# Other slots for the mixing stage's steps, and a half-chunk grid with narrow splits for the hybrid-head stage

## The reference

```
first block, per layer:
  h = h + 0.5 * rms_norm(swiglu(rms_norm(h)))            # width 2816
  u = rms_norm(h);  a_b, a_c, a_x, b_u, c_qkv, d_qkv, d_f, gates = split(u @ w_in)
  y_a = (a_b * conv3(a_c * a_x)) @ w_a                   # short convolution
  y_b = silu(layer_norm(conv31(glu(b_u)) + b)) @ w_b     # 31 taps, depthwise
  y_c = differential attention(c_qkv), 4 heads x 2 maps, rms_norm per head, @ w_c
  y_d = forgetting attention(d_qkv, cumsum(log_sigmoid(d_f))), 8 heads, @ w_d
  h = h + rms_norm((sum of sigmoid(gate_i) * y_i) @ w_o)
  h = h + 0.5 * rms_norm(swiglu(rms_norm(h)))
second block ("hybrid heads"), per layer:
  z = rms_norm(h) @ w_in                                 # 2656 columns
  a: 6 query, 2 key heads, rms_norm per head, axial rope, dense attention
  b: 6 query, 2 key heads, rope, window of 128 and a sink
  c: latents of 192 and 128, normed, times w_uq and w_ukv, 4 heads of 64 + 32 rope
  h = h + (concat(a, b, c) * silu(gates)) @ w_out
result: rms_norm(h)
```

## Time and profile before

| | |
|---|---|
| median of 3 runs | 1870.01 us (1867.84 to 1870.3) |
| profiled execution | 1870.01 us, its span 1868.2 us |
| PE busy | 1731.6 us, 93% of the span |
| DVE busy | 1125.2 us, 60% |
| ACT busy | 794.7 us, 43% |
| mean granted TensorE clock | 0.961 |

### The profile page before, as it was taken

How to read it: one execution, slowest core, us unless ns; L and a number is a source line. 1 busy time by engine, 2 the same in 40 slices (tenths; PEclk the granted TensorE clock), 3 DMA queues, 4 the chain that set the end, 5 groups by cost and what they waited for, 6 DMA issues and landing times.

```text
span 1868.2 us, 28467 instructions
## 1 busy us (share of the span) xinstructions
PE 1731.6 (93%) x12340; PEld 1614.7 (86%) x12340; DVE 1125.2 (60%) x1317; ACT 794.7 (43%) x1011; POOL 41.1 (2%) x64
## 2 busy tenths in 40 slices
PE   7999988888999999999998888899999998889886
PEld 6999888878999999899988778899999997669765
DVE  5444666766766544744466676676545476647663
ACT  5334544333444443543363443344534444434532
POOL 0000000000000000000000000000000010001000
PEclk9999999989999999999999998999999999889978
DMA  7555543433455555555454332354655452215310
GB/s 280 182 184 188 193 181 122 150 113 136 159 180 203 183 192 189 190 192 188 181 199 162 136 139 110 137 179 158 220 186 181 180 210 96 88 59 203 113 45 23
DMA packets 43357, 299.43 MB, mean 160 GB/s; under 512 B 4816, under 2 KB 5216, under 8 KB 8416
## 3 DMA queue, kind: packets, MB, share of 16 engines
q1 hardware_dynamic: 39744, 285.23, 42.2%
q10 hardware_dynamic: 3488, 12.38, 1.9%
HBM read 296.52 MB, written 1.06 MB: 159 GB/s over the span
## 4 chain that ended last, share of the span: by engine, by line
PE 74%; DVE 10%; ACT 8%; issue 5%; DVEq 3%; POOL 1%; DMA 1%; POOLq 0%; ACTq 0%; SPq 0%
PE ps L1373 21%; PE ps L1374 21%; PE ps L1375 21%; DVE wlo L838 3%; ACT whi L536 3%; PE ps L1744 2%; PE ps L1771 2%; DVEq L1119 1%; ACT prob L726 1%; ACT prob L808 1%; PE ps L1459 1%; PE ps L1755 1%; POOL rs L497 1%; PE ps L1460 1%; PE ps L1417 1%
## 5 line engine op out<-in xcount | busy, mean ns | idle before, releaser
L838 DVE TENSOR_TENSOR wlo<-raw,whi 128x2048 fp32r<-128x2048 f32 x270 | 616.8, 2291 | 474.8 <-ACT whi L536 468.2
L1373 PE MATMUL ps<-xhi,whi 128*128 128x256 f32 (+1 forms) x2512 | 724.6, 288 | 0.0
L1374 PE MATMUL ps<-xlo,whi 128*128 128x256 f32 (+1 forms) x2512 | 716.9, 285 | 0.0
L1375 PE MATMUL ps<-xhi,wlo 128*128 128x256 f32 (+1 forms) x2512 | 716.5, 285 | 0.0
L536 ACT ACTIVATE whi<-raw 128x2048 fp32r<-128x2048 f32 x270 | 508.2, 1905 | 17.5 <-DMA raw<-stream 17.0
L1373 PEld LDWEIGHTS ps<-xhi,whi 128*128 128x128 f32 (+1 forms) x2512 | 487.1, 194 | 6.2 <-issue 2.9
L1374 PEld LDWEIGHTS ps<-xlo,whi 128*128 128x128 f32 (+1 forms) x2512 | 486.7, 194 | 3.1 <-issue 0.6
L1375 PEld LDWEIGHTS ps<-xhi,wlo 128*128 128x128 f32 (+1 forms) x2512 | 486.0, 193 | 0.4
L1373 PE MATMUL ps<-whi,yar 128*128 128x512 f32 (+1 forms) x492 | 195.9, 398 | 0.7 <-DVE wlo L838 0.7
L1374 PE MATMUL ps<-wlo,yar 128*128 128x512 f32 (+1 forms) x492 | 192.1, 391 | 0.0
L1375 PE MATMUL ps<-whi,yar 128*128 128x512 f32 (+1 forms) x492 | 191.6, 389 | 0.0
(11 more groups left out here) (203 smaller groups left out, 1745.5 us busy)
## 6 DMA issues: line engine op xcount, KB each, us to landing
raw<-stream SPq DMA_DIRECT2D x270, 1024.0 KB, 4.8
gpre<-pre_gain ACTq DMA_DIRECT2D x9, 512.0 KB, 4.2
gpost<-post_gain ACTq DMA_DIRECT2D x6, 512.0 KB, 5.3
mix<-cum ACTq DMA_DIRECT2D x2, 1024.0 KB, 6.7
h<-x_in SPq DMA_DIRECT2D x2, 512.0 KB, 5.9
out<-mix SPq DMA_DIRECT2D x4, 256.0 KB, 2.1
cst<-cst_in ACTq DMA_DIRECT2D x1, 704.0 KB, 11.8
cst<-cst_in ACTq DMA_DIRECT2D x1, 576.0 KB, 5.7
```

What stands on the lines that cost most here:

```text
L838: TT(wlo[:, s, :], raw[:, s, :], whi[:, s, :].bitcast(F32), ALU.subtract).then_inc(lo_v, 1)
L1373: pe.matmul(dst, lh, rh, start=first, stop=False)
L1374: pe.matmul(dst, lh, rl, start=False, stop=False)
L1375: return pe.matmul(dst, ll, rh, start=False, stop=last)
```

## The change

It has two parts. **Mixing stage:** the load order `COLS` brings chunk 22 (the forget logits) to slot 6, and most steps get other slots: the 31 taps are spread over slots 6 to 33 instead of 6 to 36, so three slots hold two of them; the f_ steps come earlier, the attention groups and flips at other distances, the layer norm steps two slots earlier. Branch c's output moves out of `thb`. **Hybrid stage:** the table is now in half chunks (28 halves and four output steps), chunks 5, 6, 7 come before 3 and 4 (`HCOLS`), DVE's split is a step of its own (`split`, in the second half of each slot, two chunks ahead), all splits and loads take only the columns that a chunk uses (`chunk_width`: 1536, 1280, 768 or 512 of 2048), ACT takes over squares, the copies of chunks 2, 4, 7 and the value copies, the rotations take fewer instructions, group 9 has no buffers of its own, w_out's first token half is accumulated in banks 0 and 1 chunk by chunk, and the norms' scratch has columns of its own.

```diff
-COLS = (14, 15, 0, 1, 2, 3, 10, 11, 12, 13, 22, 4, 5, 6, 7, 8, 9, 16, 17, 18, 19, 20, 21)
+COLS = (14, 15, 0, 1, 2, 3, 22, 10, 11, 12, 13, 4, 5, 6, 7, 8, 9, 16, 17, 18, 19, 20, 21)
+HCOLS = (0, 1, 2, 5, 6, 7, 3, 4, 8, 9, 10, 11, 12, 13)
...
-        at(6 + tap, "conv", tap)
+        at(6 + tap * 28 // B_CONV, "conv", tap)
...
-    for g, s in enumerate((10, 12, 15, 17, 21, 24, 26, 29)):
+    for g, s in enumerate((12, 14, 16, 18, 22, 24, 27, 29)):
         at(s, "scores", g)
         at(s + 1, "weigh", g)
         at(s + 2, "turn", g)
         at(s + 3, "values", g)
...
-HYB_V = (2, 4, 7) + GATES
+HYB_V = GATES
...
+SLOTS2 = ((5.5, 6.5), (6.5, 7.5), (7.5, 8), (8, 9), (9, 10), (10, 10.5), (10.5, 11.5), (11.5, 13), (13, 14), (14, 15))
...
+    for g, (a, b) in enumerate(SLOTS2):
+        at(a, "scores", g)
+        at(a, "exp", g)
+        at(a, "weigh", g)
+        at(b, "turn", g)
+        at(b, "values", g)
...
+    for p in range(1, 15):
+        at(p + 0.5, "split", p + 2)
...
+        def acc_bank(X, t):
+            return 4 * t if X >= 3 * DEPTH else 4 + 2 * t
...
-                sp.dma_start(raw[:, c % SLOTS, :], stream[LOAD[c]]).then_inc(landed[c % SLOTS], 16)
+                w = chunk_width(c)
+                sp.dma_start(raw[:, c % SLOTS, 0:w], stream[LOAD[c]][:, 0:w]).then_inc(landed[c % SLOTS], 16)
...
-                A(whi[:, s, :], raw[:, s, :], ACT.Copy).then_inc(hi_ready, 1)
+                w = chunk_width(ch)
+                A(whi[:, s, 0:w], raw[:, s, 0:w], ACT.Copy).then_inc(hi_ready, 1)
...
+                    elif kind == "values":
+                        g = step[1]
+                        br, t, kv, ne = group(g)
+                        if br < 2:
+                            act.wait_ge(o_done, l * GROUPS2 + (8 * DEPTH + g + 1))
+                            rows_ = slice(64 * kv, 64 * kv + 64)
+                            A(oAB[rows_, 3 * br:3 * br + 3, t * P:(t + 1) * P],
+                              bank(3)[rows_, 0:3 * P].rearrange("p (m t) -> p m t", m=3), ACT.Copy).then_inc(o_read, 1)
...
-                            TT(prob[:, 0:ne, :], sc, win[:, t, :].unsqueeze(1).to_broadcast([P, ne, T]), ALU.add)
+                            far = slice((1 - t) * P, (2 - t) * P)
+                            TT(sc[:, :, far], sc[:, :, far], win[:, t, far].unsqueeze(1).to_broadcast([P, ne, P]), ALU.add)
...
-                        if turned:
+                        if turned and w == 1 and t == 1:
                             pe.wait_ge(y_ready, l * 4 + turned)
...
+                    if kind == "out":
+                        j = step[1]
+                        ready(wo[j])
+                        pe.wait_ge(y_ready, l * 3 + (4 * DEPTH + (1, 2, 2, 3)[j]))
...
+                        _, p, i, half = step
+                        c = ch + p
+                        if p < 2 or half and i in (AT_UQ, AT_UKV):
                             continue
-                        ready(c)
+                        if half == 0:
+                            ready(c)
+                            hyb_free(pe, l, p)
```

More of the change, by code:

```diff
@@ L180, in at @@
     def at(slot, *step):
[L181 to L191, removed]
+        before.setdefault(int(2 * slot), []).append(step)
+    at(3, "a_norm")
+    at(4.5, "flip", 0)
+    at(5, "flip", 1)
+    at(6, "b_rotate")
+    at(8.5, "flip", 2)
+    at(8.5, "flip", 3)
+    at(8, "l_norm")
+    at(9.5, "l_turn")
     at(11, "cq_rotate")
     at(12, "ck_rotate")
[L194 to L199, removed]
-    at(12, "o_gate", 0)
-    at(15, "o_gate", 1)
-    at(17, "o_gate", 2)
-    rank = {"flip": 0, "l_turn": 0, "turn": 1, "scores": 2, "exp": 2, "values": 3, "weigh": 4}
-    steps = []
[L205 to L208, removed]
+    at(12, "flip", 4)
+    at(12, "flip", 5)
+    at(12.5, "flip", 6)
+    at(12.5, "flip", 7)
+    for g, (a, b) in enumerate(SLOTS2):
[4 more added lines that the diff above has]
+        at(b, "values", g)
+    at(12, "o_gate", 0)
+    at(14, "o_gate", 1)
+    at(15.5, "o_gate", 2)
+    for p in range(1, 15):
+        at(p + 0.5, "split", p + 2)
+    rank = {"flip": 0, "l_turn": 0, "turn": 1, "scores": 2, "exp": 2, "values": 3, "split": 7, "weigh": 8}
+    steps = []
+    for half in range(2 * AT_WOUT + 4):
+        steps += sorted(before.pop(half, []), key=lambda x: rank.get(x[0], 6))
+        if half < 2 * AT_WOUT:
+            steps.append(("chunk", half // 2, HCOLS[half // 2], half % 2))
+        else:
+            steps.append(("out", half - 2 * AT_WOUT))
     assert not before, before
@@ L572, in boundary @@
                     squares_acc(X, ch, 1, 0)
+                else:
+                    split(ch + 1)
                 if not last:
@@ L862, in boundary @@
                 split(ch)
-                split(ch + 1)
-                per = 4 if share else 2
                 if share:
+                    split(ch + 1)
                     dve.wait_ge(gpost_in, X * 16 + 16)
@@ L875, in boundary @@
                                 dve.wait_ge(sq_done, q + (4 * t + 1))
-                            STT(out=thb[:, half], in0=bank(4 + 2 * t + n), scalar=share, in1=gpost[:, half], op0=ALU.mult,
+                            STT(out=thb[:, half], in0=bank(acc_bank(X, t) + n), scalar=share, in1=gpost[:, half], op0=ALU.mult,
                                 op1=ALU.mult)
@@ L1204, in _ @@
+                dve.drain()
                 for step in HYB:
                     kind = step[0]
-                    if kind == "chunk":
-                        i = step[1]
-                        c = ch + i
-                        if i in GATES:
+                    if kind == "split":
+                        split(ch + step[1])
+                    elif kind == "chunk":
+                        _, p, i, half = step
+                        c = ch + p
+                        if i in GATES and half:
@@ L1420, in turns, with rows_of, rows_tail @@
                         ins.then_inc(xt_done, 1)
-            def rows_tail(X, chs, lhs, lls, wait, last=False):
+            def rows_of(X, ch, lh, ll, t, final, first, last=False):
+                s = ch % SLOTS
+                wh, wl = wts(whi, s, 2), wts(wlo, s, 2)
+                for a in range(2):
+                    if final and t and a and not last:
+                        turns(X + 1, 0)
+                    for b in range(2):
+                        n, k = (a, b) if final else (b, a)
+                        ins = mm3(bank(acc_bank(X, t) + n), lh[:, k, t * P:(t + 1) * P], ll[:, k, t * P:(t + 1) * P],
+                                  wh[:, k, n * 512:(n + 1) * 512], wl[:, k, n * 512:(n + 1) * 512], first and k == 0,
+                                  final and b == 1)
+                    if final and not (t and a):
+                        ins.then_inc(acc_done, 1)
+                if t:
+                    ins.then_inc(used, 1)
+            def rows_tail(X, chs, lhs, lls, wait):
                 for t in range(NT):
@@ L1665, in _, with banks_free @@
                 token_pair(ch, X, Z_CHUNKS[0])
+                wo = [ch + AT_WOUT + i for i in range(4)]
+                def banks_free(step, wanted):
+                    at = HYB.index(step)
+                    for b in wanted:
+                        users = [x for x in HYB[:at] if x[0] == "l_turn" or x[0] == "flip" and 2 + x[1] % 2 == b
+                                 or x[0] == "values" and b == 3]
+                        if not users:
+                            continue
+                        if users[-1][0] == "l_turn":
+                            pe.wait_ge(lat_ready, l + 1)
+                        elif users[-1][0] == "flip":
+                            pe.wait_ge(qkt_a, l * 8 + (users[-1][1] + 1))
+                        else:
+                            pe.wait_ge(o_read, l * GROUPS2 + (8 * DEPTH + users[-1][1] + 1))
```

342 lines of the change are left out of this document (168 added, 174 removed).

## The result

The changed kernel takes 1796.66 us (median of 4, 1791.93 to 1797.79), the one before 1869.4 us (median of 4, 1867.84 to 1870.3). The ratio is 0.9607, with a 95% interval of 0.9588 to 0.9625: 73 us less, where 1800 us was forecast. The profiled execution took 1796.47 us, its span is 1794.7.

What follows compares the result with a forecast made beforehand. PE was taken as the bound: its matmuls, its waits and the time a lowered clock adds. Gains of 42 us in two mixing layers and 28 in two hybrid layers, 70 from 1870.0, gave 1800 us, range 1760 to 1832.

Steps and rivals of the forecast that it cites:

- the clock's share: Time PE loses to a lowered clock before the change: 11 us per mixing layer, 12 per hybrid layer.
- The mixing layer, 43 to 22: Mixing layer's idle time plus clock loss falls from 43 us to 22: 21 won, 42 in two layers.
- turn 2: Mixing stage, slot 17: PE waits 5.0 us because DVE is behind with `weigh` and the read of `values` 1.
- turn 3: Mixing stage, after slots 17 and 18: PE waits 5.8 us, from full DVE slots plus 3.7 waiting for ACT.
- gate: Mixing stage, slot 23: the first gate waits 4.4 us for ACT's copy of slot 22's chunk to free bank 0.
- The hybrid layer, 37 to 22: Hybrid layer's idle time plus clock loss falls from 37 us to 22: 14 to 15 won, 28 in two layers.
- ukv: Hybrid stage: this chunk waits 3.9 us for ACT's copy of uq, which stands behind exp 6.
- turns 3 and 5: Hybrid stage: new PE waits of 1.0 us each at these two turns.
- The waits dissolve: Rival, both stages: a quarter of the new waits remains, with most low clock gone; 1762 us, chance 0.25.
- Only the mixing stage pays: Rival, hybrid stage: uq, ukv and the end eat the hybrid gain; 1828 us, chance 0.13.
- ScalarE becomes the bound: Rival, hybrid layers: ACT's added work makes later chunks wait for their banks; 1879 us, slower, chance 0.03.
- The hybrid clock stays low: Rival, hybrid stage: small transposes and score products keep the clock low, 12 us stay; 1810 us, chance 0.08.

Runs made afterwards that it cites:

- e7: Changed kernel with ACT's exps of groups 2 to 4 and o_norm behind their slot's copy and split, and no taps in slots 15 to 19: 1758.21 us.
- e6: Changed kernel with the convolution taps moved out of slots 15 to 19, more of them in slots 6 to 11: 1787.53 us.
- e2: Changed kernel with the mixing stage's edits taken back, so only the hybrid part is changed: 1837.08 us.
- e8: Changed kernel with the edits of e7 and e4, and w_out's last split on DVE moved to slot 14.5: 1746.58 us.
- e4: Changed kernel with ACT's copies of the uq and ukv chunks, and the split behind, moved to their slot's first half: 1790.66 us.

## Why the prediction was right

**What can be won.** I had put the clock's share of a mixing layer at 11 us and its idle time at 32, so 43 to win. e7 shows the floor: at a clock of 1.00 the layer's matmuls take PE 318.3 us, and before it was busy 329.5, so the clock cost 11.3; idle was 362.2 - 329.5 = 32.7. Both terms stand.

**The mixing layer, 43 to 22.** Idle after is 339.7 - 322.8 = 16.9 in layer 0 and 15.5 in layer 1 (15.5 forecast); the clock costs 322.8 - 318.3 = 4.5 and 7.5 (6.5 forecast). Wait by wait in layer 0: turn 0 1.22 (1.1), turn 1 0.92 (0.7), turn 2 4.80 (5.0), turn 3 4.87 (5.8), gate 4.58 (4.4). The one that missed is turn 3's, by 0.9. The five add up to 16.4, between the 17.0 of the plain sum and the 15.5 that I took. My sum for turn 3 counted DVE's load beside ACT's order; e6 shows that without the load 4.7 of the 4.9 us stay.

**The hybrid layer, 37 to 22.** Idle fell from 24.6 to 164.6 - 147.6 = 17.0, where I took 15; PE's busy time fell by 6.9, where I took 5 for the clock. The two errors cancel, which is luck. The idle time came out low because I subtracted 0.3 for each of 14 waits from a list of 19 (it has 13 waits and adds up to 18.6), and because a wait of 0.86 for the norm at the layer's start, there before and after, was not on it. Of that list, ukv 3.79 (3.9), `flip` 5 2.75 (2.7), chunk 5 1.73 (1.8), out 3 1.83 (2.0) and out 1 1.26 (1.1) stand. **A step that was wrong:** turns 3 and 5 (1.0 each) do not wait at all and turn 2 only 0.48 instead of 0.9, perhaps because I counted DVE's half slots as serial where the half slot between has room, which no run tests; values 7 and 8 are 0.2 longer each. That is 2.4 us less and 0.4 more. There is luck in the total too: each part alone won more than I had for it (44.5 for 42, 32.7 for 28), while both together gave 4 us less than the two alone, of which 2.3 lie in hybrid layer 0 and its clock.

**The rivals.** *The waits dissolve* fell: every large one is there, within a us. That they could be dissolved, by another order, e7 shows: a mixing layer of 323.4 us, 38.8 less than before, with order changed, a buffer moved and some semaphore waits moved or weakened. *Only the mixing stage pays* fell by e2, 32.7 us. *ScalarE becomes the bound* fell: ACT is busy 80.9 of 164.6 us, and in that stage only uq's and ukv's copies hold up a chunk (3.79 and 0.46). *The hybrid clock stays low* fell: the layer's clock rose from 0.90 to 0.95, and to 0.97 in e8, while it has the same 937 PE instructions, its transposes among them. Of the 12 us that I had for the clock, PE's busy time lost 6.9 with the change and 10.6 in e8 (154.5, 147.6, 143.9). From the full change to e8 even the order of PE's instructions is the same, and only its waits differ. So most of the low clock before was due to the waits. The Trainium skill ("TensorE: Matmul & The Clock Gate", Part 4: PE-mode transpose) says that transposes do not count as work for the clock gate like other matmuls; by that rule the 12 us of the rival would have stayed, and the trace does not agree. What no run separates is whether transposes make the stage more sensitive to a short wait.

## What to carry over

When engines run in order, ask of each instruction that waits (an exp for a maximum) what is queued behind it that doesn't need it: here the copy that frees a PSUM bank and the split of the next chunk. In the mixing layers putting these ahead was worth 25 us, spreading DVE's load 6, both together 34, and in the hybrid stage narrower splits were worth nothing. Compare kernels stage by stage: the totals held another 4 to 5 us from stages whose code was the same. The account of idle time plus low clock, each read off whole stages, gave the total within 4 us, and a slot-by-slot sum gave every wait of a strict bank to 0.3 us; sums over waits that slack may absorb mostly came out too long.

## What the hardware showed that I had not expected

**Equal waits leave unequal stretches of low clock.** `turn` 2 waits 4.80 us in both mixing layers of the changed kernel. Eleven us around it in layer 0 and in layer 1, the same code:

```profile
321.00:332.00 11.00, 8.47 (x56) 7.34 (x57) 10.44 (x19) 1.08 (x2) 0.00 (x0) 0.84 0.18 73
1042.00:1053.00 11.00, 8.12 (x44) 6.99 (x45) 10.46 (x18) 1.43 (x2) 0.00 (x0) 0.69 0.19 81
```

A mean of 0.84 over 11 us, with levels of 1 and 1/2, is 3.5 us at 1.2 GHz; 0.69 is 6.8. PE then comes 1.1 us later to `turn` 3 in layer 1 and waits 1.1 us less there (3.79 for 4.87). Around that turn the means are 0.84 and 0.69 again, so the shorter wait has the longer stretch. Two times 3.3 us more at 1.2 GHz, half of it lost, are about what layer 1 lost more to the clock than layer 0 (7.5 us for 4.5).

**The same short wait was followed by low clock in one kernel and not in another.** Two stretches of 8 us of the changed kernel: `values` 4 waited 1.04 us in the hybrid stage, and turn 0 waited 1.22 us in the mixing stage:

```profile
1543.00:1551.00 8.00, 6.96 (x22) 4.22 (x21) 3.80 (x9) 4.26 (x10) 0.00 (x0) 0.79 0.41 131
289.00:297.00 8.00, 6.78 (x58) 6.29 (x57) 7.45 (x14) 0.71 (x2) 0.00 (x0) 1.00 0.36 131
```

The first is at 0.79, the second at 1.00. The kind of work ahead of the wait doesn't explain it: in e7 `values` 4 waits the same 1.04 us with the same code around it, and its 8 us (1506.7 to 1514.7) are at 1.00. Chunk 5's wait of 1.73 us is alike: the 18 us around it are at 0.91 in the changed kernel (1486.7 to 1504.7) and at 1.00 in e7 (1451.8 to 1469.8). It takes no other chip: e2 and e4 ran on the same one, and the same 18 us are at 1.00 in e2 (1530.5 to 1548.5) and at 0.91 in e4 (1486.9 to 1504.9). And turn 0's wait of 1.56 was followed by 0.79 over 8 us in e8 and by 1.00 in e7. What decides it is open. It makes the same hybrid layer take 168.8 us in one kernel and 165.8 in another, with the code unchanged, which is as much as some of the edits above won.
